# Linear attention in a two-layer backbone: the key-value product of each head on its own 64 columns of TensorE, both heads at the same PSUM columns

## The chip, the cores and the metric

The kernel runs on one core of a Trainium2 chip. The metric is device time in microseconds from the first to the last instruction of the program, with the small fixed part around them; a run's time is compared with other runs on the same chip. TensorE (PE) multiplies, VectorE (DVE) and ScalarE (ACT) work elementwise and read PSUM, GpSimd (POOL) works elementwise in SBUF, SyncE (SP) issues most of the loads.

## The reference, cut to what matters

Two layers over 512 latent and 256 context tokens. Each layer is a half-step feed-forward network, a token mixer and a second feed-forward network. One branch of the mixer is gated linear attention with 4 heads (key width 64, value width 128), in chunks of 64 tokens, forwards and backwards:

```python
kv = jnp.einsum('bhncd,bhnce->bhnde', k_end, vc)      # per head and chunk: (64 x 64 tokens) x (64 tokens x 128)
decay = jnp.exp(b_last[:, :, :, 0, :])

def step(s, inp):
    kv_n, dec_n = inp
    return s * dec_n[..., None] + kv_n, s
```

The state of a head is 64 x 128 numbers. The chain of 12 chunks (8 of the latent, 4 of the context) is walked in order, so each state needs the one before it.

## The kernel before

All values are float32. The large products (feed-forward, projections) are split into a high and a low part in float32r (`whi`, `wlo`, `hhi`, `hlo`) and run at lines 1261 and 1268. One "unit" is 128 output columns over all tokens. The attention's small products are plain float32; each such `matmul` appears in the trace as two MATMUL and two LDWEIGHTS records.

Attention handles the heads in two pairs (`pr` 0 and 1), for each of 2 layers. Head `h` of the pair lies on partitions 64h to 64h+63 of `states`, `dec` and `kt`. A pair needs `KV_STEPS` = 11 state steps. In step `s`, for each of the 2 directions `d`:

- `kv_products` on PE multiplies the two heads' keys of one chunk (`kpad`, 128 columns: 64 for each head) with the two heads' values (`vt`, 256 columns: 128 for each head). Of the 128 x 256 result only two blocks are wanted: head 0's keys with head 0's values (partitions 0 to 63, columns 0 to 127), and head 1's with head 1's (partitions 64 to 127, columns 128 to 255). The other half is computed and never read.
- `state_step` on DVE makes the next state from each block, with one instruction for each head and direction: 4 per step. They are line 1070 for `s` = 0 and line 1072 after it.

PSUM is double-buffered: step `s` uses bank `s % 2`, so PE may run two steps ahead of DVE and then waits for `kv_used`. The other attention products are the scores (`scores`, line 692, masked by DVE at 1054 and 1055), the outputs (`outputs`, line 712, copied by ACT at 906) and transposes of values (line 605, drained by DVE's `copy_v` at 1006) and of decayed keys (line 672, drained by ACT at 879 and 880).

The order is written out by hand for each engine. On PE the small products are a generator, `gla_tensor`, whose pieces are placed by `gla_slot` between the k-chunks of 8 large units, `fill_tensor`. Each engine executes in program order, so a PE piece that waits also holds the large units behind it. On DVE, `gla_vector` puts between the state steps: `scale_keys` (1047, `kt`), `scale_queries` (1029, `qbd`), `copy_v`, `mask_scores` and the split of the next unit's weights (1703, `wlo`). For pair 1, `scores(1, 0)` is PE's next attention piece after `kv_products(1, 7)` and waits for the last of the four `scale_queries`, which DVE issues after state step 6.

Of the kernel before, what the change touches and what calls it, by code (L numbers as in the profile page):

```python
# [21 lines left out]
P = 128  # L22
# [9 lines left out]
DK = 64  # L32
DV = 128
# [38 lines left out]
ALU = mybir.AluOpType  # L72
# [88 lines left out]
def blocks(l):  # L161
    return NBLK if l < DEPTH - 1 else XBLK


def gla_slot(l, kind, pr=0, i=0):


    lead, chain, out = (5, (1.3, 1.8), 1.5) if l < DEPTH - 1 else (8, (1.6, 2), 2)
    chains = [lead + 4, 0]
    outs = [chains[0] + chain[0] * KV_STEPS + 1, 0]  # L170
    chains[1] = outs[0] + 2 * out * blocks(l) + 1
    outs[1] = chains[1] + chain[1] * KV_STEPS + 1
    if kind == "kend":
        return lead + i / 2 if pr == 0 else outs[0] + 2 * out * (1 + i / 2) + out / 2
    if kind == "kv":
        return chains[pr] + chain[pr] * i
    if kind == "o":
        return outs[pr] + 2 * out * i
    assert kind == "var"
    return outs[1] + 2 * out * (2 + i if i < 2 else blocks(l) + i / 2)  # L180
# [13 lines left out]
def build(nc, t):  # L194
# [87 lines left out]
    vt = lay("vt", [P, NBLK, VW])  # L282
    kq = lay("kq", [P, 4, NT])
    states = lay("states", [P, 2, NCH, DV])
    bsum = lay("bsum", [P, 4, NT])
    qbd = lay("qbd", [P, 2, 2, NT])
    kpad = lay("kpad", [P, 2, NBLK, 2, P])
# [6 lines left out]
    dec = lay("dec", [P, 2, NCH])  # L294
# [31 lines left out]
    ps = ctx.enter_context(nc.psum_tensor("ps", [P, 8 * 512], F32))  # L326

    def bank(b, c0=0, n=512):
        return ps[:, 512 * b + c0:512 * b + c0 + n]
# [115 lines left out]
    def at_least(eng, s, value):  # L445

        if not isinstance(value, int) or value > 0:
            eng.wait_ge(s, value)
# [199 lines left out]
    def o_before(l, pr):  # L648

        return 2 * sum(blocks(i) for i in range(l)) + pr * blocks(l)  # L650
# [8 lines left out]
    def gla_tensor(pe, l, p0):  # L659
# [15 lines left out]
        def kv_products(pr, s):  # L675

            kv0 = (2 * l + pr) * KV_STEPS
            at_least(pe, kv_used, kv0 + s - 1)
            for d, order in enumerate((FWD, BWD)):
                c = order[s]  # L680
                mm = nc.tensor.matmul(bank(s % 2, d * 2 * P, 2 * P), kpad[:, d, c // 2, c % 2, :],  # L681
                                      vt[:, c // 2, 2 * pr * DV:2 * (pr + 1) * DV], start=True, stop=True)
            mm.then_inc(kv_ready, 1)

        def scores(pr, b):
# [318 lines left out]
    def copy_v(dve, l, g):  # L1004
        dve.wait_ge(misc_ready, MISC * l + 5 + g)
        nc.vector.tensor_copy(vt[:, :, g * DV:(g + 1) * DV],
                              bank(6, 0, NT).rearrange("p (b n) -> p b n", b=NBLK)).then_inc(misc_free, 1)

    def to_end(dve, l, pr):

        dve.wait_ge(b_ready, 4 * l + 2 * pr + 2)
        if pr:
            dve.wait_ge(eq_ready, 4 * l + 2)
        for d in range(2):
            b = bsum[:, 2 * pr + d, :].rearrange("p (n c) -> p n c", c=CHUNK)
            e = (CHUNK - 1, 0)[d]
            nc.vector.tensor_tensor(kend(pr)[:, d, :].rearrange("p (n c) -> p n c", c=CHUNK),
                                    b[:, :, e:e + 1].to_broadcast([P, NCH, CHUNK]), b, ALU.subtract).then_inc(d_ready, 1)

    def scale_kend(dve, l, pr):  # L1020
        for d in range(2):
            dve.wait_ge(eend_ready, 4 * l + 2 * pr + d + 1)
            nc.vector.tensor_tensor(kend(pr)[:, d, :], kq[:, pr, :], kend(pr)[:, d, :], ALU.mult).then_inc(kend_ready, 1)

    def scale_queries(dve, l, pr, d, h):
        c = blocks(l) * P
        dve.wait_ge(eq_ready, 4 * l + 2 * pr + d + 1)
        r = slice(h * DK, (h + 1) * DK)
        ins = nc.vector.tensor_tensor(qbd[r, d, h, 0:c], kq[r, 2 + pr, 0:c], qbd[r, d, h, 0:c], ALU.mult)
        if h:  # L1030
            ins.then_inc(prep_ready, 1)

    def gla_vector(dve, steps, l, u0, split_lo):
        nb = blocks(l)
        done = 0

        def fill_to(slot):

            nonlocal done
            while done < FILL and SLOTS * (done + 1) + 1 <= slot:  # L1040
                unit = u0 + AHEAD + done + 2
                split_lo(unit, unit % 4, unit % 2)
                done += 1

        def scale_keys(pr, d):
            dve.wait_ge(ekt_ready, 4 * l + 2 * pr + d + 1)
            nc.vector.tensor_tensor(kt[:, d, :], kq[:, pr, :], kt[:, d, :], ALU.mult)

        def mask_scores(pr, b):
            ob = o_before(l, pr)  # L1050
            dve.wait_ge(s_ready, ob + b + 1)

            at_least(dve, o_ready, ob + b - 1)
            steps.link(nc.vector.copy_predicated(att[:, b % 2, :], masks[:, 0, :], bank(6 + b % 2, 0, 2 * P)))
            nc.vector.copy_predicated(att[:, b % 2, :], masks[:, 1, :],
                                      bank(6 + b % 2, 2 * P, 2 * P)).then_inc(att_ready, 1)

        def state_step(pr, s):
            kv0 = (2 * l + pr) * KV_STEPS
            dve.wait_ge(kv_ready, kv0 + s + 1)  # L1060
            if s:
                dve.wait_ge(kv_used, kv0 + s)
            for d, order in enumerate((FWD, BWD)):
                ch, nxt = order[s], order[s + 1]
                for h in range(2):
                    r = slice(h * DK, (h + 1) * DK)
                    col = 512 * (s % 2) + d * 2 * P + h * DV
                    kv = ps[r, col:col + DV]
                    if s == 0:
                        ins = nc.vector.tensor_copy(states[r, d, nxt, :], kv)  # L1070
                    else:
                        ins = nc.vector.scalar_tensor_tensor(  # L1072
                            out=states[r, d, nxt, :], in0=states[r, d, ch, :], scalar=dec[r, d, ch:ch + 1],
                            in1=kv, op0=ALU.mult, op1=ALU.add)
            ins.then_inc(kv_used, 1)

        unit = u0 + AHEAD + 1
        split_lo(unit, unit % 4, unit % 2)
        scale_keys(0, 0)
        scale_queries(dve, l, 0, 1, 0)  # L1080
        scale_queries(dve, l, 0, 1, 1)
        dve.wait_ge(dec_ready, 2 * l + 1)
        for s in range(KV_STEPS):
            fill_to(gla_slot(l, "kv", 0, s))
            state_step(0, s)
            if s == 1:
                scale_keys(0, 1)
            if s in (2, 3):
                copy_v(dve, l, s)
            if s in (5, 6):  # L1090
                mask_scores(0, s - 5)
        to_end(dve, l, 1)
        for b in range(2, nb):
            fill_to(gla_slot(l, "o", 0, b - 1.5))
            mask_scores(0, b)
            if b == 2:
                scale_kend(dve, l, 1)
        fill_to(gla_slot(l, "o", 0, nb - 1))
        dve.wait_ge(o_ready, o_before(l, 0) + nb)
        dve.wait_ge(dec_ready, 2 * l + 2)  # L1100
        for s in range(KV_STEPS):
            fill_to(gla_slot(l, "kv", 1, s))
            state_step(1, s)
            if s in (1, 2):
                scale_keys(1, s - 1)
            if 3 <= s <= 6:
                scale_queries(dve, l, 1, (s - 3) // 2, (s - 3) % 2)
            if s == 8:
                mask_scores(1, 0)
        mask_scores(1, 1)  # L1110
        for b in range(2, nb):
            fill_to(gla_slot(l, "o", 1, b - 1.5))
            mask_scores(1, b)
        fill_to(gla_slot(l, "var", 1, HEADS - 1))
        dve.wait_ge(ostd_ready, l + 1)
        v = tok[:].rearrange("p (h b) -> p h b", h=HEADS)[:, :, 0:nb]
        nc.vector.reciprocal(v, v).then_inc(orec_ready, 1)
        fill_to(NEVER)
# [1079 lines left out]
```

## Time and profile before

| | |
|---|---|
| median of 3 runs | 3025.59 us (3024.77 to 3027.01) |
| profiled execution, its own time | 3025.89 us |
| its span | 3024.1 us |
| PE busy | 2961.8 us (98%) |
| DVE busy | 1599.1 us (53%) |
| ACT, POOL busy | 830.5 us (27%), 259.6 us (9%) |
| state step instructions (1070 and 1072) | 16 + 160, 288 and 348 ns median |
| key-value MATMUL records (681) | 176, 379 ns median |

A record's duration is its own, from start to end; consecutive matmuls overlap, so what a matmul costs PE is the distance from one start to the next. Only where PE is idle inside a stretch does the work of another engine reach the end of the program. Attention of layer 0 lies at 716 to 860 us of the span, that of layer 1 at 2345 to 2460 us.

### The profile page before, as it was taken

How to read it: one execution, taken by the hardware profiler on the slowest of the kernel's cores; microseconds unless marked ns; L12 is line 12 of the kernel's file. 1: busy time of each engine (PE TensorE's matmuls, PEld its weight loads, DVE VectorE, ACT ScalarE, POOL GpSimd, SP SyncE). 2: the span in 40 equal slices, each digit the busy share in tenths (PEclk: the TensorE clock that was granted, in tenths of full speed). 3: DMA queues.
4: the chain of work that ended last, by engine and by line, in shares of the span. 5: the costliest groups of instructions: out<-in, count | busy, mean ns of one | idle time of the engine just before them, and what ended most of it. 6: DMA issues, size and time to landing. Idle time of an engine off the chain costs nothing.

```text
span 3024.1 us, 41524 instructions
## 1 busy us (share of the span) xinstructions
PE 2961.8 (98%) x16228; PEld 2537.2 (84%) x16228; DVE 1599.1 (53%) x2658; ACT 830.5 (27%) x1142; POOL 259.6 (9%) x260
## 2 busy tenths in 40 slices
PE   7999999999999999999999999999999899999998
PEld 5888888888888888888888888888888688888886
DVE  6676776557443348776765752222245744433333
ACT  4211211243232232212112421121234333432223
POOL 2000000112600020000000200000021500200001
PEclk8999999999999999999999999999999999999998
DMA  6444334222012224434442432222113123333331
GB/s 215 119 118 133 118 112 140 70 59 50 25 49 62 70 70 134 137 112 132 118 133 70 119 91 63 63 62 63 53 40 85 39 65 96 91 96 92 98 94 65
DMA packets 455618, 273.64 MB, mean 90 GB/s; under 512 B 9754, under 2 KB 453828, under 8 KB 455492
## 3 DMA queue, kind: packets, MB, share of 16 engines
q1 hardware_dynamic: 453348, 267.90, 31.1%
q10 hardware_dynamic: 2144, 4.00, 0.4%
q8 instruction: 87, 1.43, 0.2%
q14 instruction: 39, 0.32, 0.0%
HBM read 269.77 MB, written 2.10 MB: 90 GB/s over the span
## 4 chain that ended last, share of the span: by engine, by line
PE 91%; DVE 4%; ACT 2%; issue 1%; DMA 0%; SPq 0%; POOL 0%; DVEq 0%; ACTq 0%; POOLq 0%
PE ps L1261 54%; PE ps L1268 27%; PE ps L1436 2%; PE ps L1284 2%; PE ps L1441 1%; DVE states L1072 1%; PE ps L712 1%; PE ps L1318 1%; PE ps L681 1%; DVE first_acc L1770 1%; PE ps L692 1%; ACT hhi L1601 0%; DMA first_mod<-in_w_mod 0%; DVE hlo L1826 0%; PE ps L596 0%
## 5 line engine op out<-in xcount | busy, mean ns | idle before, releaser
L1261 PE MATMUL ps<-hhi,whi 128*128 128x512 f32 x3136 | 890.7, 351 | 0.2 <-ACT whi L1530 0.2
L1261 PE MATMUL ps<-hlo,whi 128*128 128x512 f32 x3136 | 879.6, 348 | 0.0
L1703 DVE TENSOR_TENSOR wlo<-wraw,whi 128x1024 fp32r<-128x1024 f32 x371 | 456.8, 1232 | 594.1 <-ACT whi L1530 591.4
L1530 ACT ACTIVATE whi<-wraw 128x1024 fp32r<-128x1024 f32 x371 | 391.4, 1056 | 932.6 <-PE ps L1268 908.3
L1268 PE MATMUL ps<-hhi,wlo 128*128 128x512 f32 x3136 | 629.9, 350 | 0.0
L1261 PEld LDWEIGHTS ps<-hhi,whi 128*128 128x128 f32 x3136 | 501.3, 188 | 82.4 <-issue 3.1
L1268 PEld LDWEIGHTS ps<-hhi,wlo 128*128 128x128 f32 x3136 | 501.5, 188 | 80.6 <-issue 1.0
L1261 PEld LDWEIGHTS ps<-hlo,whi 128*128 128x128 f32 x3136 | 500.3, 188 | 79.8 <-issue 0.5
L1717 DVE SCALAR_TENSOR_TENSOR macc<-modraw,cond,macc 128x256 f32<-128x256 f32 x896 | 366.2, 478 | 0.1
L1261 PE MATMUL ps<-mhi,whi 128*128 128x512 f32 (+1 forms) x1184 | 333.8, 349 | 4.2 <-DVE mlo L1967 2.9
L1261 PE MATMUL ps<-mlo,whi 128*128 128x512 f32 (+1 forms) x1184 | 332.2, 348 | 0.0
L1963 DVE TENSOR_TENSOR mtmp<-ps,stmp 128x512 f32<-128x512 f32 (+1 forms) x154 | 82.6, 572 | 303.6 <-ACT stmp L1654 303.6
L1268 PE MATMUL ps<-mhi,wlo 128*128 128x512 f32 (+1 forms) x1184 | 234.5, 348 | 0.0
L1654 ACT ACTIVATE stmp<-ps 128x512 f32<-128x512 f32 (+1 forms) x154 | 70.8, 505 | 555.6 <-PE ps L1268 555.6
L1261 PEld LDWEIGHTS ps<-mhi,whi 128*128 128x128 f32 x1184 | 188.8, 188 | 37.3 <-DVE mlo L1967 5.0
L1268 PEld LDWEIGHTS ps<-mhi,wlo 128*128 128x128 f32 x1184 | 189.0, 188 | 30.6
L1261 PEld LDWEIGHTS ps<-mlo,whi 128*128 128x128 f32 x1184 | 188.9, 188 | 30.3
L2111 POOL MEMSET ssq<- 128x768 f32 x7 | 5.2, 741 | 2225.4 <-PE ps L1268 1856.1
L1977 DVE SCALAR_TENSOR_TENSOR x<-ps,gate,x 128x512 f32<-128x512 f32 (+3 forms) x156 | 89.9, 635 | 148.1 <-PE ps L1268 148.1
L1967 DVE TENSOR_TENSOR mlo<-mtmp,mhi 128x768 f32 (+3 forms) x88 | 78.5, 892 | 91.2 <-ACT mhi L1658 91.2
L1658 ACT ACTIVATE mhi<-mtmp 128x768 f32 (+3 forms) x88 | 69.8, 793 | 107.9 <-DVE mtmp L1963 107.9
L2021 POOL TENSOR_TENSOR ssq<-ssq,sq 128x768 f32<-128x768 f32 (+2 forms) x52 | 83.6, 1609 | 164.6 <-ACT sq L1555 81.5
(193 smaller groups left out, 2377.8 us busy)
## 6 DMA issues: line engine op xcount, KB each, us to landing
wraw<-in_ffn_up SPq DMA_DIRECT2D x176, 512.0 KB, 3.9
modraw<-in_w_mod SPq DMA_DIRECT2D x66, 1024.0 KB, 5.2
wraw<-in_ffn_down SPq DMA_DIRECT2D x64, 512.0 KB, 3.7
wraw<-in_w_in SPq DMA_DIRECT2D x64, 512.0 KB, 4.0
wraw<-in_ffn_down SPq DMA_DIRECT2D x32, 384.0 KB, 3.3
wraw<-in_w_out SPq DMA_DIRECT2D x16, 512.0 KB, 3.7
first_mod<-in_w_mod SPq DMA_DIRECT2D x6, 1024.0 KB, 12.5
wraw<-in_w_br_pool SPq DMA_DIRECT2D x16, 256.0 KB, 2.8
```

The source lines that it names most:

```text
L1261: nc.tensor.matmul(o, whi[:, slot, k, :], a[:, k * NT + t0:k * NT + t0 + n], start=(k == 0 and a is hi), stop=False)
L1268: mm = nc.tensor.matmul(o, wlo[:, slot, k, :], hi[:, k * NT + t0:k * NT + t0 + n], start=False, stop=k == kk - 1)
L1284: mm = nc.tensor.matmul(o, w[:, (unit + s) % 2, k, :], h[:, k * NT + t0:k * NT + t0 + n], start=(k == 0 and w is whi and h is hhi and open ...
L1530: nc.scalar.activation(whi[:, slot2], wraw[:, slot4], ACT.Copy).then_inc(hi_split, 1)
L1654: ins = nc.scalar.activation(stmp[:, h, pt[0]:pt[0] + pt[1]], pair_ps(buf, 0, pt), ACT.Silu)
L1658: nc.scalar.activation(mhi[:, ds((2 * i + h) * NT, c)], mtmp[:, h, 0:c], ACT.Copy).then_inc(mhi_done, 1)
L1703: nc.vector.tensor_tensor(wlo[:, slot2], wraw[:, slot4], whi[:, slot2].bitcast(F32), ALU.subtract).then_inc(lo_split, 1)
L1717: ins = nc.vector.scalar_tensor_tensor(out=macc[:, buf, c, :], in0=modraw[:, buf, k, :], scalar=cond[:, c * DC + k:c * DC + k + 1], in1=ma ...
L1963: ins = nc.vector.tensor_tensor(mtmp[:, h, pt[0]:pt[0] + pt[1]], pair_ps(buf, 1, pt), stmp[:, h, pt[0]:pt[0] + pt[1]], ALU.mult)
L1967: nc.vector.tensor_tensor(mlo[:, ds((2 * i + h) * NT, c)], mtmp[:, h, 0:c], mhi[:, ds((2 * i + h) * NT, c)].bitcast(F32), ALU.subtract).th ...
L1977: ins = nc.vector.scalar_tensor_tensor(out=x[:, ds(n * NT + t0, m)], in0=pair_ps(buf, s, (t0, m)), scalar=gate[:, ds(e * DC + n, 1)], in1= ...
L2021: nc.gpsimd.tensor_tensor(ssq[:, t0:t0 + c], ssq[:, t0:t0 + c], sq[:, j % 2, t0:t0 + c], ALU.add).then_inc(sq_used, 1)
```

## The change

On PE, the product of a direction becomes two, one for each head: 64 of the key columns with that head's own 128 value columns, written to that head's 64 partitions of PSUM, at the same 128 columns for both heads. On DVE, both blocks of a direction then lie at the same columns on all 128 partitions, and one instruction handles both heads.

```diff
@@ kv_products
             for d, order in enumerate((FWD, BWD)):
                 c = order[s]
-                mm = nc.tensor.matmul(bank(s % 2, d * 2 * P, 2 * P), kpad[:, d, c // 2, c % 2, :],
-                                      vt[:, c // 2, 2 * pr * DV:2 * (pr + 1) * DV], start=True, stop=True)
+                for h in range(2):
+                    r = slice(h * DK, (h + 1) * DK)
+                    mm = nc.tensor.matmul(bank(s % 2, d * DV, DV)[r], kpad[:, d, c // 2, c % 2, r],
+                                          vt[:, c // 2, (2 * pr + h) * DV:(2 * pr + h + 1) * DV], start=True, stop=True)
             mm.then_inc(kv_ready, 1)
@@ state_step
                 ch, nxt = order[s], order[s + 1]
-                for h in range(2):
-                    r = slice(h * DK, (h + 1) * DK)
-                    col = 512 * (s % 2) + d * 2 * P + h * DV
-                    kv = ps[r, col:col + DV]
-                    if s == 0:
-                        ins = nc.vector.tensor_copy(states[r, d, nxt, :], kv)
-                    else:
-                        ins = nc.vector.scalar_tensor_tensor(
-                            out=states[r, d, nxt, :], in0=states[r, d, ch, :], scalar=dec[r, d, ch:ch + 1],
-                            in1=kv, op0=ALU.mult, op1=ALU.add)
+                kv = bank(s % 2, d * DV, DV)
+                if s == 0:
+                    ins = nc.vector.tensor_copy(states[:, d, nxt, :], kv)
+                else:
+                    ins = nc.vector.scalar_tensor_tensor(
+                        out=states[:, d, nxt, :], in0=states[:, d, ch, :], scalar=dec[:, d, ch:ch + 1],
+                        in1=kv, op0=ALU.mult, op1=ALU.add)
             ins.then_inc(kv_used, 1)
```

DVE in layer 0, pair 1, from state step 0 to the last `scale_queries`, before (`states` and `kt`, `qbd` are the tiles that are written; 64x128 is partitions by columns; x4 is four instructions in a row):

```order
L1070 COPY states<-ps 64x128 x4
L1072 SCALAR_TENSOR_TENSOR states<-states,dec,ps 64x128 x4
L1047 TENSOR_TENSOR kt<-kq,kt 128x768
L1072 SCALAR_TENSOR_TENSOR states<-states,dec,ps 64x128 x4
L1029 TENSOR_TENSOR qbd<-kq,qbd 64x768
L1703 TENSOR_TENSOR wlo<-wraw,whi 128x1024
```

The same rows of the change:

```order
L1069 COPY states<-ps 128x128 x2
L1071 SCALAR_TENSOR_TENSOR states<-states,dec,ps 128x128 x2
L1049 TENSOR_TENSOR kt<-kq,kt 128x768
L1071 SCALAR_TENSOR_TENSOR states<-states,dec,ps 128x128 x2
L1031 TENSOR_TENSOR qbd<-kq,qbd 64x768
L1702 TENSOR_TENSOR wlo<-wraw,whi 128x1024
```

Nothing changes its place in the order; every state step is two instructions on 128 partitions where it was four on 64.

PE in layer 0, pair 0, around state steps 1 to 3, before (64x128 or 128x256 is the result, partitions by columns):

```order
L1261 MATMUL ps<-hlo,whi 128x256
L681 MATMUL ps<-vt,kpad 128x256 x4
L605 MATMUL ps<-ident,vf 128x128 x6
L1261 MATMUL ps<-hhi,whi 128x512
L681 MATMUL ps<-vt,kpad 128x256 x2
```

The same rows of the change:

```order
L1260 MATMUL ps<-hlo,whi 128x256
L683 MATMUL ps<-vt,kpad 64x128 x8
L605 MATMUL ps<-ident,vf 128x128 x6
L1260 MATMUL ps<-hhi,whi 128x512
L683 MATMUL ps<-vt,kpad 64x128 x4
```

A step's two matmuls become four, each with half the moving columns and half the stationary ones, between the same neighbours, all of which use the full 128 x 128 array.

## Rows read from the trace of the kernel before

**Rows 1.** The page: its head, and the chain that ended last, by engine.
```profile
span 3024.1 us, 41524 instructions
...
PE 91%; DVE 4%; ACT 2%; issue 1%; DMA 0%; SPq 0%; POOL 0%; DVEq 0%; ACTq 0%; POOLq 0%
```

**Rows 2.** Timeline of PE, layer 0 pair 1: start, duration, instructions, [idle before <-releaser].
```profile
781.86 1.13 PE L681 MATMUL ps<-vt,kpad 128*128 128x256 f32 x4 [0.18 <-DVE states L1072]
...
786.09 1.13 PE L681 MATMUL ps<-vt,kpad 128*128 128x256 f32 x4 [1.70 <-DVE states L1072]
...
788.42 1.13 PE L681 MATMUL ps<-vt,kpad 128*128 128x256 f32 x4 [0.51 <-DVE states L1072]
792.06 1.46 PE L692 MATMUL ps<-qbd,kt 128*128 128x256 f32 x4 [2.50 <-DVE qbd L1029]
792.96 3.12 PE L1268 MATMUL ps<-hhi,wlo 128*128 128x512 f32 x8
...
796.66 1.06 PE L1268 MATMUL ps<-hhi,wlo 128*128 128x512 f32 x4
```

**Rows 3.** Stretch after them: busy PE, PEld, DVE, ACT, POOL, clock, DMA.
```profile
792.00:796.70 4.70, 4.64 (x17) 3.97 (x17) 1.33 (x4) 0.00 (x0) 3.88 (x12) 0.64 0.01 2
```

**Rows 4.** Timeline of DVE, layer 0 pair 1.
```profile
774.22 1.43 DVE L1072 SCALAR_TENSOR_TENSOR states<-states,dec,ps 64x128 f32<-64x128 f32 x4 [0.98 <-PE ps L681]
775.69 1.70 DVE L1047 TENSOR_TENSOR kt<-kq,kt 128x768 f32<-128x768 f32 x1
...
788.40 0.98 DVE L1029 TENSOR_TENSOR qbd<-kq,qbd 64x768 f32<-64x768 f32 x1
...
790.74 1.18 DVE L1029 TENSOR_TENSOR qbd<-kq,qbd 64x768 f32<-64x768 f32 x1
```

**Rows 5.** Line 1072, who waited for it: us in all, times (whole program).
```profile
  PE ps L681: 5.6, 7
```

**Rows 6.** Timeline of PE, its other idle times in the two attention stretches.
```profile
726.97 0.87 PE L605 MATMUL ps<-ident,vf 128*128 128x128 f32 x6 [1.86 <-DVE vt L1006]
...
752.74 0.52 PE L672 MATMUL ps<-ident,bsum 128*128 128x128 f32 x3 [0.45 <-DVE bsum L1023]
...
2356.19 0.88 PE L605 MATMUL ps<-ident,vf 128*128 128x128 f32 x6 [2.11 <-DVE vt L1006]
...
2373.88 0.71 PE L712 MATMUL ps<-att,vt 128*128 128x128 f32 x4 [2.27 <-DVE states L1072]
...
2412.72 1.10 PE L692 MATMUL ps<-qbd,kt 128*128 128x256 f32 x4 [2.82 <-DVE qbd L1029]
```

**Rows 7.** Timeline of DVE, layer 1 pair 1: step 1, last query scaling.
```profile
2396.72 1.43 DVE L1072 SCALAR_TENSOR_TENSOR states<-states,dec,ps 64x128 f32<-64x128 f32 x4
...
2410.92 1.65 DVE L1029 TENSOR_TENSOR qbd<-kq,qbd 64x512 f32<-64x512 f32 x1
```

**Rows 8.** The chain that ended last, in order of time: start, duration, what.
```profile
737.92 0.86 PE ps L681 x4
738.78 0.70 PE ps L1268 x4
```

**Rows 9.** Timeline of PE around products on 32 columns (128*32), line 1342.
```profile
203.21 0.52 PE L1268 MATMUL ps<-mhi,wlo 128*128 128x512 f32 x2
203.65 0.28 PE L1342 MATMUL ps<-mred,fold 128*32 128x24 f32 x8
203.86 0.62 PE L1261 MATMUL ps<-mhi,whi 128*128 128x512 f32 x2
204.31 0.52 PE L1261 MATMUL ps<-mlo,whi 128*128 128x512 f32 x2
204.67 0.52 PE L1261 MATMUL ps<-mhi,whi 128*128 128x512 f32 x2
```

**Rows 10.** Timeline of DVE before the first state step.
```profile
715.71 0.95 DVE L1047 TENSOR_TENSOR kt<-kq,kt 128x768 f32<-128x768 f32 x1
716.58 1.91 DVE L1029 TENSOR_TENSOR qbd<-kq,qbd 64x768 f32<-64x768 f32 x2
```

## The prediction

> **What bounds the kernel now.** I read the page first: the chain that ended last is 91% PE and 4% DVE [rows 1]. PE is therefore the bound nearly everywhere, and an edit to DVE counts only where PE stands idle for it. Then I asked for the line of the state steps and who waits for it: PE's key-value products wait 5.6 us in 7 places [rows 5]. That is only the direct part, so I went through PE's timeline in both attention stretches for each idle time, and through DVE's for what made it late.
>
> In layer 0, pair 1, PE waits 0.18, 1.70 and 0.51 us for line 1072 and 2.50 us for the scaled queries [rows 2], 4.9 us together. DVE has no gap from 774.22 to 791.92 us [rows 4], and in that stretch lie the state steps 1 to 6, at 1.43 us each. Layer 1, pair 1 looks the same: of the 5.6 us in 7 places [rows 5], what is left after the three of layer 0 is 3.2 us, in four places. To it comes 2.82 us before the scores [rows 6], 6.0 us together, while DVE is occupied from 2396.72 to 2412.57 us, again with six state steps inside [rows 7]. Four further idle times stand in [rows 6]: 1.86 and 2.11 us for the copy of transposed values, 0.45 us for a scaled key, and 2.27 us for the last state of pair 0 in layer 1. All of PE's idle time that has DVE behind it is thus 4.9 + 6.0 + 1.86 + 0.45 + 2.11 + 2.27 = 17.6 us.
>
> One more cost hangs on it. Right after the 2.50 us wait the granted clock averages 0.64 over 792.0 to 796.7 us [rows 3], so part of that stretch runs at 1.2 instead of 2.4 GHz. From the start of the scores at 792.06 to 796.66 us [rows 2] PE does four records of scores, eight of line 1268 and four of key-value products. At full clock these take 0.86 + 1.40 + 0.86 = 3.1 us (a key-value group of four is 0.86 and four of line 1268 are 0.70 [rows 8]; the scores have the form of the key-value products). It took 4.6 us, so the slow clock costs 1.4 to 1.5 us. Layer 1 has the same shape after its 2.82 us wait, and I put it at 1.4 us too.
>
> **DVE: four instructions become two.** 1.43 us for four is 0.358 us each. The new ones have the same 128 columns but twice the partitions. Does that cost time? 128x768 took 0.95 us, and two of 64x768 took 1.91 us, 0.955 each [rows 10]: partitions cost nothing. So a step falls from 1.43 to 0.72 us, by 0.72 us.
>
> A bound on the better side: the instructions of [rows 10] overlap, the second starts at 716.58, 0.08 us before the first ends at 716.66, whereas the state instructions stand 0.358 us apart with durations of 0.348. If the new pair and its successor overlap as those do, another 0.1 us is gained at each of two places, and a step saves 0.9 us. The Trainium skill (VectorE: DVE Perf Modes, section Two Vector instructions with no wait between them) says that an instruction is held until all earlier ones have finished when its operands start in another quadrant of partitions than those of the instruction before. The old steps alternate between partitions 0 and 64 and would all be held, the new ones would not; by the page the saving would be about 0.9 us, by the bare count of instructions 0.72. I take between 0.72 and 0.9, nearer to the count, since a step's first instruction also follows a wait.
>
> What this is worth, place by place:
> - Layer 0 pair 1: six steps save 4.3 to 5.4 us of DVE's chain; PE's idle time there is 4.9 us, and the fresh weight load after each of four waits adds 0.1 (1.13 instead of about 1.03 us). I take 4.6.
> - Layer 1 pair 1: six steps again, 6.0 us of idle time: 4.6.
> - The two waits for copied values, 1.86 and 2.11 us: state steps 1 and 2 lie on DVE between the first products and the copy, 1.43 to 1.8 us saved. I take 1.5 each, 3.0.
> - The last state of pair 0, layer 1, 2.27 us: the last four steps follow each other on DVE almost without gap and would save 2.9 us. All of the wait goes, 2.3 with its weight load.
> - The scaled key, 0.45 us: it is late by the last state step (0.7 us shorter). I take 0.4.
> - The clock: remaining waits before the scores would be 1 us or less in layer 0 and about 1.5 in layer 1. At 2.11 and 2.27 us [rows 6] no slow stretch follows in this trace, only after 2.50 and 2.82. So I count both stretches as gone, 2.8 us.
>
> Sum: 4.6 + 4.6 + 3.0 + 2.3 + 0.4 + 2.8 = 17.7 us.
>
> **PE: two matmuls become four on half the columns.** Before, a step costs 0.86 us for four records of 256 columns, 0.215 each [rows 8], so 128 columns are 0.107. After it there are eight records of 128 columns. One after another they are 0.86 us again. If the two 64-column halves of the array work side by side, they are 0.43; if records start in program order, with head 0's two and then head 1's two, a head's first can only run beside the other's second, and a step is five times 0.107, 0.54.
>
> To this comes going to half the array and back. The trace has the nearest case in line 1342 [rows 9], eight records on 32 columns between full-array products. A pair of large matmuls is normally 0.36 us (204.31 to 204.67), so line 1342 should have started at 203.57 and started at 203.65: 0.08 to 0.09 to get in. From there to line 1261 it is 0.21. Back on the full array the first pair takes 0.45 instead of 0.36: 0.09. In all 0.39 us, of which the 24 moving columns can hardly be more than 0.04 when side by side. Eight loads and eight products one after another would be 8 x (32 + 24) columns at 0.84 ns, 0.38 us, and they and the way out took 0.21: the column groups do overlap. The rest, 0.35 us, I take for the two switches, plus 0.03 for loading 64 columns first instead of 32.
>
> The Trainium skill (TensorEngine Tiling (Array Packing), section Tiling Modes, Key Properties) says both things: changing the tiling mode drains TensorE, which speaks against this change, and tiles load and multiply in parallel, which speaks for it. By these rows the trace agrees with both.
>
> So a step costs 0.38 plus 0.43, 0.54 or 0.86 us: 0.81, 0.92 or 1.24, against 0.86. I take 0.92, since that is what in-order starts give: +0.06 us, 2.6 us over 44 steps. Some 12 steps lie where PE waits for DVE anyway and hides it, which leaves 2 us. If that cover were gone the full 2.6 would count. Nothing else changes: no load, no other wait, and no instruction moves past another.
>
> Total: 17.7 - 2 = 15.7 us. Against the profiled execution, 3025.89 - 15.7 = 3010.2; its time is 0.3 above the median, so 3010 us.
>
> **The rivals.**
> - **The halves of the array do not overlap.** The float32 records of one head then follow those of the other, and a step costs 1.24 us, +0.38. With 32 steps in the open that is 12.2 us, and 17.7 - 12.2 = 5.5 gained: 3020. Against it stands line 1342 [rows 9], but with 32 columns and short products. Chance 0.12.
> - **The gain is passed on to another wait.** PE comes to each later place earlier, and ACT's drains of the transposed keys or GpSimd (which slows DVE's kt to 1.70 us where 0.95 is usual [rows 4, 10]) now hold it; and one of the slow stretches of the clock stays or comes elsewhere. If half of the DVE terms (7.5) and one slow stretch (1.4) are lost, the gain is 6.8: 3019. For it speaks that layer 1 pair 1 keeps 1.5 us of waiting even by my count. Chance 0.08.
> - **Slower: weight loads are exposed.** If with half the columns each load has to wait for the product in front of it, each of a step's eight adds 0.05 us (half of the 0.1 seen after a wait [rows 2]). A step costs 0.38 + 0.86 + 0.43 = 1.67 us, +0.81; over 32 steps 26 us, less 17.7: 3034. This ends above the old time as soon as a step costs more than 17.7 / 32 = 0.55 us extra. The Trainium skill (TensorE: Matmul & The Clock Gate, Part 3, What overlaps and what doesn't) has loads overlap running products only when their row groups differ, and here they are the same; the full-array rows, all with the same row group, already contradict it, with a float32 product of 128 columns and its load at 0.107 us. Chance 0.06.
> - **More than forecast.** Side-by-side halves (0.81 a step, 2 us better than before), state steps at 0.9 and all 17.6 us of waits gone: 17.6 + 1 + 2.8 + 2 = 23.4, 3002. Chance 0.12, at the edge of my own case.
>
> **How the numbers follow.** My case, 3004 to 3016, has 0.62 and gives the forecast of 3010. The 3002 case and the two cases at 3019 and 3020 are taken into the range, 3002 to 3020; the exposed loads and what lies beyond the others are left out. 0.2% is 6 us, about what a measurement of this kernel can tell from no change, so faster means below 3019.5. My case, the better one and half of the two weaker ones give 0.84; the other half gives 0.10 for no change; slower has 0.06.
>
> **What would show it.** The state steps of the changed kernel should stand as x2 on 128 partitions at about 0.35 us each, 0.7 a step or less. The 2.50 and 2.82 us waits before the scores should be below 1 and 1.6 us, and the wait for the last state of pair 0 in layer 1 gone. The clock should read 1.00 after them. A step of key-value products between two large ones should cost PE about 0.92 us from start to start; 1.24 would show the first rival, 1.6 the third. The prediction is wrong if that distance is above 1.4, or if PE's waits name ACT where they named DVE.

## The result, and the profile after

The changed kernel took 2999.49 us (median of 4 runs, 2998.74 to 3000.08), the kernel before, beside it, 3026.24 us (4 runs, 3024.77 to 3027.01). The ratio is 0.9911, 95% interval 0.9899 to 0.9923: 26.8 us or 0.9% faster. The forecast was 15.7 us faster and its range ended at 3002: right in direction and outside the range by 2.5 us.

The page of the changed kernel, head and chain by engine (line numbers are one lower or two higher than before):

```profile
span 2997.0 us, 41788 instructions
...
PE 93%; DVE 3%; ACT 2%; issue 1%; DMA 0%; SPq 0%; POOL 0%; DVEq 0%; ACTq 0%; POOLq 0%
```

DVE's share of the chain fell from 4% [rows 1] to 3%, and PE's grew from 91% to 93% of a shorter span. The next view is PE's timeline of the changed kernel, its idle times in the attention stretches (they answer [rows 2, 6]):

```profile
724.56 0.88 PE L605 MATMUL ps<-ident,vf 128*128 128x128 f32 x6 [0.42 <-DVE vt L1008]
...
749.77 0.52 PE L672 MATMUL ps<-ident,bsum 128*128 128x128 f32 x3 [0.45 <-ACT kpad L882]
...
783.19 1.10 PE L694 MATMUL ps<-qbd,kt 128*128 128x256 f32 x4 [0.57 <-DVE qbd L1031]
...
2342.04 0.87 PE L605 MATMUL ps<-ident,vf 128*128 128x128 f32 x6 [0.51 <-DVE vt L1008]
...
2388.98 1.10 PE L694 MATMUL ps<-qbd,kt 128*128 128x256 f32 x4 [1.57 <-DVE qbd L1031]
```

The waits of 2.50 and 2.82 us before the scores are now 0.57 and 1.57; the copies of values went from 1.86 and 2.11 to 0.42 and 0.51; the wait for the last state, 2.27 us, has no row any more. PE's key-value products have no wait for a state left in the trace, where they had seven, 5.6 us together [rows 5]. Only the 0.45 us at line 672 is as before, and there the name has changed: it was DVE's `bsum`, it is now ACT's `kpad`.

To see where the time went, both attention stretches are cut from the first transposed key (line 672) to the first spread of the norm (line 780, now 782). Stretches by window, PE alone: length, busy, records, clock, DMA. First the kernel before, then the changed one:

```profile
713.93:857.03 143.10, 135.45 (x791) 0.99 0.13 32
2344.31:2455.06 110.75, 98.99 (x495) 0.98 0.17 41
```

```profile
713.85:846.33 132.48, 130.59 (x878) 1.00 0.14 35
2332.29:2429.53 97.24, 93.68 (x584) 1.00 0.18 47
```

The two together went from 253.9 to 229.7 us: 24.1 of the 27.1 us by which the spans differ. PE's idle time in them went from 19.4 to 5.5 us. What is left, 3.0 us, lies outside, where both programs are the same. One thing that differs there is the clock. Two windows in other phases, in the kernel before and then in the changed one:

```profile
1675.00:1690.00 15.00, 15.00 (x105) 0.89 0.01 1
2238.00:2260.00 22.00, 22.00 (x131) 0.84 0.04 8
```

```profile
1675.00:1690.00 15.00, 14.99 (x98) 1.00 0.54 150
2238.00:2260.00 22.00, 21.97 (x147) 1.00 0.00 1
```

The windows do not hold quite the same work, but no slow stretch of the clock shows near these places in the changed kernel (1.00 over 1650 to 1700 and over 2205 to 2250 us). At a mean of 0.84 over 22 us, 3.5 us' worth of clock is missing, and at 0.89 over 15 us another 1.7. The 3.0 us are a net figure, though. The changed kernel leaves the attention of layer 0 10.7 us ahead (857.03 against 846.33) and is only 8.4 us ahead 200 us later (PE's rows at 1057.13 and 1048.70). It then gains 1.6 and 3.1 us where the two slow stretches are missing, loses 1.0 in other places, and enters the attention of layer 1 12.0 us ahead (2344.31 against 2332.29). The last 1.6 us are gained behind that. Most of the 2.3 us goes where the large products follow each other at another rate: by their starts from 950 to 1040 us, about 0.174 us a record in the kernel before and 0.176 to 0.177 in the changed one. No run here explains that.

The new pair of state instructions, DVE's timeline (it answers [rows 4]):

```profile
770.90 0.61 DVE L1071 SCALAR_TENSOR_TENSOR states<-states,dec,ps 128x128 f32<-128x128 f32 x2 [1.60 <-PE ps L683]
771.43 1.50 DVE L1049 TENSOR_TENSOR kt<-kq,kt 128x768 f32<-128x768 f32 x1
```

Two instructions take 0.61 us, and the next starts 0.08 us before they end, 0.53 us after the first began. The four of before held DVE for 1.47 us (774.22 to 775.69). A step saves 0.94 us. And the step of products, from the chain that ended last (it answers [rows 8]) and PE's timeline:

```profile
736.71 0.59 PE ps L683 x8
737.30 0.89 PE ps L1267 x4
```

```profile
735.15 0.66 PE L683 MATMUL ps<-vt,kpad 128*64 128x128 f32 x8
735.74 0.97 PE L1267 MATMUL ps<-hhi,wlo 128*128 128x512 f32 x4
736.64 0.66 PE L683 MATMUL ps<-vt,kpad 128*64 128x128 f32 x8
```

The period is 1.49 us with four records of line 1267, which need 0.70 behind full-array products [rows 8] and 0.89 behind half-array ones. With everything above 0.70 put down to the step, it costs 0.79 us: 0.07 less than the 0.86 of before, where the forecast said 0.06 more.

### The profile page after: what moved, and what is told of

It reads as the page before. It is cut to its first block, busy times and chain, and to the rows that moved or that the text cites. A ratio compares the mean times of both kernels' runs of the same rounds, so it can differ in the third digit from the quotient of the medians.

```text
span 2997.0 us, 41788 instructions
## 1 busy us (share of the span) xinstructions
PE 2949.3 (98%) x16404; PEld 2515.6 (84%) x16404; DVE 1563.6 (52%) x2570; ACT 830.4 (28%) x1142; POOL 262.6 (9%) x260
## 4 chain that ended last, share of the span: by engine, by line
PE 93%; DVE 3%; ACT 2%; issue 1%; DMA 0%; SPq 0%; POOL 0%; DVEq 0%; ACTq 0%; POOLq 0%
PE ps L1260 55%; PE ps L1267 28%; PE ps L1435 2%; PE ps L1283 2%; PE ps L1440 1%; PE ps L714 1%; PE ps L694 1%; DVE first_acc L1769 1%; PE ps L1317 1%; PE ps L683 1%; ACT hhi L1600 0%; DMA first_mod<-in_w_mod 0%; DVE hlo L1825 0%; PE ps L596 0%; DVE x L1976 0%
## 6 DMA issues: line engine op xcount, KB each, us to landing
first_mod<-in_w_mod SPq DMA_DIRECT2D x6, 1024.0 KB, 12.2
```

## The experiments

Each was run beside the kernel before on the same chip. "Attention" is the sum of the two stretches cut as above, from PE's timeline in that kernel's profile (before 253.9, changed 229.7). It comes from one execution of each kernel, while the times are medians.

**The PE half alone.** DVE keeps four instructions; each head keeps its own PSUM columns.

```diff
-                mm = nc.tensor.matmul(bank(s % 2, d * 2 * P, 2 * P), kpad[:, d, c // 2, c % 2, :],
-                                      vt[:, c // 2, 2 * pr * DV:2 * (pr + 1) * DV], start=True, stop=True)
+                for h in range(2):
+                    r = slice(h * DK, (h + 1) * DK)
+                    mm = nc.tensor.matmul(bank(s % 2, d * 2 * P + h * DV, DV)[r], kpad[:, d, c // 2, c % 2, r],
+                                          vt[:, c // 2, (2 * pr + h) * DV:(2 * pr + h + 1) * DV], start=True, stop=True)
```

> Only the PE half of the change: two matmuls per direction on 64 columns each, but each head keeps its own PSUM columns and DVE its four instructions per step. Theory A (the changed trace: a step costs PE 0.79 us where it was 0.86, and nearly all the rest of the gain is DVE's): 32 steps in the open times 0.07 is 2.4 us, so 3022 to 3025 us, with the waits for states as long as before and both slow clock stretches in attention still there. Theory B (PE's part is a large share of the 27 us): below 3018. The prediction's own term (0.92 a step, 2 us lost): 3028.

3028.49 us (10 runs, 3021.14 to 3033.07), ratio 1.0003 (0.9993 to 1.0012): no difference. Both theories missed; the 3028 of the prediction's own term is met by luck, since a step costs 0.79 us and not the 0.92 behind it. In the profiled execution (3029.7 us, above the median) attention took 259.2 us, 5 us more than before, although each step of products is as short as in the change. The windows of the two stretches in this kernel:

```profile
714.18:859.13 144.95, 135.65 (x878) 0.95 0.13 32
2344.67:2458.87 114.20, 99.73 (x584) 0.94 0.16 40
```

PE is idle 23.8 us here against 19.4 before: DVE's chain sets the time, and a faster PE only waits longer. And the clock is lower: 2 x (0.05 x 145 + 0.06 x 114) is some 28 us at 1.2 GHz, against 7 before. PE's busy time is 235.4 us, where the changed kernel needs 224.3 for the same 878 and 584 records, 11 us less. At half speed 28 us cost 14, but some 5 of the 28 fall on waits and cost nothing there (from 789.5 to 796.5 us the clock is 0.51 and PE is busy for 4.0 of 7.0 us), which leaves 11 to 12. Against before, 4.4 us went into waits, and the 3 that the steps save were more than eaten by the clock.

**The DVE half alone.** PE keeps its two products of 128 x 256. The one instruction per direction reads the first 128 columns on all 128 partitions, so head 1's state is made from head 0's values: the computation is changed there, and the work has the same size.

```diff
-                for h in range(2):
...
-                        ins = nc.vector.scalar_tensor_tensor(
-                            out=states[r, d, nxt, :], in0=states[r, d, ch, :], scalar=dec[r, d, ch:ch + 1],
-                            in1=kv, op0=ALU.mult, op1=ALU.add)
+                kv = bank(s % 2, d * 2 * P, DV)
...
+                    ins = nc.vector.scalar_tensor_tensor(
+                        out=states[:, d, nxt, :], in0=states[:, d, ch, :], scalar=dec[:, d, ch:ch + 1],
+                        in1=kv, op0=ALU.mult, op1=ALU.add)
```

> Only the DVE half: PE's products as before (128 x 256), DVE two instructions of 128 partitions per step. For head 1 it reads head 0's value columns, so the states of head 1 are computed from the wrong block; amounts of work are those of the change. Theory A: everything but PE's 2 to 3 us is here, 3001 to 3004 us, a state step takes 0.60 us, waits before the scores below 2 us. Theory B (the two halves work only together, or PE's part is large): 3010 or more.

3003.87 us (4 runs, 2998.51 to 3007.58), ratio 0.992 (0.9903 to 0.9937): theory A. Attention is 232.9 us (PE busy for 228.6 of it). The DVE half is 20.9 of the 24.1 us there, and the PE half, worth nothing alone, adds 3.2 on top of it: close to 44 x 0.07. That is read from profiles; the intervals of the two times (0.9903 to 0.9937 and 0.9899 to 0.9923) overlap.

**Both heads on the same half of the array.**

```diff
-                    mm = nc.tensor.matmul(bank(s % 2, d * DV, DV)[r], kpad[:, d, c // 2, c % 2, r],
+                    mm = nc.tensor.matmul(bank(s % 2, d * 2 * P + h * DV, DV)[0:DK], kpad[:, d, c // 2, c % 2, r],
```

> The change, but both heads' products go to the same 64 columns of the array (partitions 0 to 63 of PSUM, side by side in columns), so that they cannot run beside each other; DVE's instructions are those of the change and for head 1 read partitions that no product has written. Theory A (the two halves of the array run fully beside each other, eight records in 0.43 us): here they are one after another, a step costs PE about 1.22 instead of 0.79 us, and with 32 of 44 steps in the open the time is 3011 to 3016. Rival (short products are not bound by the array, so no overlap was gained): within 2 us of the change, 2998 to 3002.

3018.69 us (9 runs, 3014.53 to 3020.49), ratio 0.997 (0.996 to 0.998). PE's timeline:

```profile
739.00 1.09 PE L683 MATMUL ps<-vt,kpad 128*64 128x128 f32 x8
740.02 0.97 PE L1267 MATMUL ps<-hhi,wlo 128*128 128x512 f32 x4
740.91 1.09 PE L683 MATMUL ps<-vt,kpad 128*64 128x128 f32 x8
```

The period is 1.91 us, so a step costs 1.21: 0.42 more than in the change, which is 4 x 0.107. Attention is 245.1 us, 15.4 more. The halves run fully side by side in the change, and without that two thirds of the gain would be gone: this is the first rival of the prediction (3020), made on purpose. DVE reads partitions here that no product has written, so the results differ and the work does not.

**PE's two loops exchanged.**

```diff
-            for d, order in enumerate((FWD, BWD)):
-                for h in range(2):
+            for h in range(2):
+                for d, order in enumerate((FWD, BWD)):
```

> The change with PE's two loops exchanged: both directions of head 0 first, then both of head 1. Theory A, in the strict form that records start in program order (behind the prediction's 0.54): four records of one half stand ahead of the first of the other, a step costs about 7 x 0.107 + 0.36 = 1.11 us, 3008 to 3012. Rival (each half takes its own records as it comes free, as the records 7 ns apart in the trace of the change suggest): 0.79 as in the change, 2998 to 3001.

3003.74 us (4 runs, 2998.19 to 3007.71), ratio 0.9915 (0.9899 to 0.9932), the same as the change within the intervals. Its timeline shows the step of the change, not the 1.11 us of starts in program order:

```profile
736.48 0.66 PE L683 MATMUL ps<-vt,kpad 128*64 128x128 f32 x8
737.07 0.97 PE L1267 MATMUL ps<-hhi,wlo 128*128 128x512 f32 x4
737.97 0.66 PE L683 MATMUL ps<-vt,kpad 128*64 128x128 f32 x8
```

**The same eight records on the full array.** The DVE half as above, and PE's product cut by value columns alone; head 1's state is again made from head 0's values.

```diff
+                for h in range(2):
+                    mm = nc.tensor.matmul(bank(s % 2, d * 2 * P + h * DV, DV), kpad[:, d, c // 2, c % 2, :],
+                                          vt[:, c // 2, (2 * pr + h) * DV:(2 * pr + h + 1) * DV], start=True, stop=True)
```

> As the change, two matmuls per direction with 128 moving columns each, but on all 128 stationary columns, so the array is never divided; DVE as in the change, reading head 0's value columns for both heads (head 1's states are computed from the wrong block). Theory A (the switch in and out of the half array costs 0.36 us a step, in the change's step of 0.79 and the one-half step of 1.21): a step costs PE 0.86 us, the time is that of the DVE half alone, 3001 to 3005. Rival (the number of records costs): above 0.95 a step, 3006 or more.

3003.28 us (4 runs, 3000.74 to 3004.46), ratio 0.9916 (0.99 to 0.9933). PE's timeline:

```profile
736.36 1.05 PE L682 MATMUL ps<-vt,kpad 128*128 128x128 f32 x8
737.17 0.94 PE L1266 MATMUL ps<-hhi,wlo 128*128 128x512 f32 x4
737.95 1.05 PE L682 MATMUL ps<-vt,kpad 128*128 128x128 f32 x8
```

Period 1.59, a step 0.89 us, and attention 233.6, like the DVE half alone. Three prices follow: eight records one after another 0.86 to 0.89; with the array divided and no overlap 1.21, so going in and out costs 0.32 to 0.35; with overlap 0.79. Running the halves side by side saves 0.43 us a step, and dividing the array costs a third of a microsecond.

**DVE's two loops exchanged, on the kernel before.**

```diff
-            for d, order in enumerate((FWD, BWD)):
-                ch, nxt = order[s], order[s + 1]
-                for h in range(2):
-                    r = slice(h * DK, (h + 1) * DK)
+            for h in range(2):
+                r = slice(h * DK, (h + 1) * DK)
+                for d, order in enumerate((FWD, BWD)):
+                    ch, nxt = order[s], order[s + 1]
```

> The kernel before with DVE's two loops exchanged: head 0's two directions, then head 1's two, four instructions as before. Theory A (an instruction starts before the end of the one ahead only when both start at the same partition): two of the four places overlap by 0.09 us, a step takes 1.26 instead of 1.43 us; two stretches of six steps give 1.0 us each and the rest 0.5, so 3023 to 3025, a slow clock stretch less perhaps. Rival (the 0.60 us of the new pair comes from something else): 1.43 a step, 3025 to 3028.

3019.67 us (7 runs, 3017.12 to 3021.47), ratio 0.9973 (0.9961 to 0.9984): 7 us for an exchange of two lines, where theory A gave 1 to 3. DVE's timeline:

```profile
738.11 1.24 DVE L1072 SCALAR_TENSOR_TENSOR states<-states,dec,ps 64x128 f32<-64x128 f32 x4
```

1.24 us where four took 1.43: two of the three seams inside a step now join instructions that start at the same partition, and each is 0.08 to 0.1 us shorter. Attention fell by 5.1 us to 248.8. Its slow clock did not shrink: in windows of half a microsecond the clock is at 1.2 GHz for 6.8 us of attention, as in the kernel before.

**Longer waits on the full array, and half-array products with shorter waits.** These two ask why the clock was so low in the attention of the PE half alone. The first is the kernel before with two short instructions more in each step on DVE:

```diff
+                        if h == 0:
+                            nc.vector.scalar_tensor_tensor(
+                                out=spare[r, d, :], in0=states[r, d, ch, 0:8], scalar=dec[r, d, ch:ch + 1],
+                                in1=kv[:, 0:8], op0=ALU.mult, op1=ALU.add)
```

> The kernel before, with two more short instructions of 8 columns on DVE in every state step after the first (their result goes to a spare tile), about 0.2 us each: a step takes DVE some 1.8 to 1.9 us instead of 1.43, PE still uses the whole array. What is asked is why the PE half alone was so slow although its step is 0.07 us shorter: its granted clock in attention was at 1.2 GHz for 27 us instead of 7. Theory A (longer waits of PE for the states bring the slow stretches, whatever form the products have): the waits grow by 0.4 us for each of some 16 steps on DVE's chain, and slow stretches in attention multiply, 3035 to 3040. Theory B (the half-array products bring the slow clock): waits grow but the slow stretches stay at about two, 3031 to 3034.

3036.86 us (5 runs, 3035.1 to 3040.87), ratio 1.0042 (1.0028 to 1.0056). A step takes DVE 1.7 us. The clock over 700 to 865 us is 0.98 and over 2330 to 2460 us 0.97, some 14 us of slow clock: twice that of before, half that of the PE half alone, whose waits for states are as long (7.3 and 7.5 us for products). The start of one of its steps on DVE also bears on the seams:

```profile
777.55 0.34 DVE L1073 SCALAR_TENSOR_TENSOR states<-states,dec,ps 64x128 f32<-64x128 f32 x1 [0.97 <-PE ps L682]
777.82 0.21 DVE L1077 SCALAR_TENSOR_TENSOR spare<-states,dec,ps 64x8 f32<-64x8 f32 x1
778.04 0.71 DVE L1073 SCALAR_TENSOR_TENSOR states<-states,dec,ps 64x128 f32<-64x128 f32 x2
```

The short instruction begins at the partition of the one before it and starts 0.07 us before that one ends; the next begins at partition 64 and starts only when the short one has ended.

The second is the PE half alone with DVE's loops exchanged as above.

> The PE half of the change with DVE's four instructions in the order of the heads (1.24 instead of 1.43 us a step): half-array products with shorter waits. Theory A (waits bring the slow clock): slow stretches in attention like those of the kernel before or fewer, and the gain over the PE half alone is more than the 7 us that this order gave on the kernel before, 3014 to 3020. Theory B (half-array products bring it): the slow stretches stay near 27 us in attention, 3021 or more.

3017.26 us (10 runs, 3015.6 to 3020.54), ratio 0.9972 (0.9962 to 0.9981), inside theory A's range. That is the ratio of the exchange on the kernel before (0.9973): the PE half was worth nothing once more, as long as PE waits for DVE. Against the PE half alone (1.0003) the exchange gave 0.3%, or 9 us, which is not clearly more than the 0.27% on the kernel before. Attention is 248.3 us, its mean clock 0.99 and 0.97.

What the profiles say of the clock is best seen side by side: PE's waits for DVE in attention, and the time at 1.2 GHz there in windows of half a microsecond:

| products | kernel | waits for DVE | at 1.2 GHz |
|---|---|---|---|
| full array | DVE's loops exchanged | 12.5 us | 7 us |
| full array | before | 17.7 us | 7 us |
| full array | two more instructions | 20.9 us | 14 us |
| half array | DVE's loops exchanged | 16.3 us | 10 us |
| half array | PE half alone | 21.9 us | 27 us |

The kernels with the longest waits have the most slow clock with either form of product, so that theory A holds in direction. Where half-array products were set beside full-array ones with about the same waits there was more of it, a half more in one case and twice as much in the other, so the form may count as well. One profile each does not separate the two.

**The change again, and what it still waits for.**

> The changed kernel itself once more, in more rounds. What is asked is how much of the 27 us is steady. In its first profile 24 us of the gain lie in the two attention stretches and 2.7 us outside them, where the program is the same and only slow clock stretches differ. Theory A (the part outside is chance, it depends on where the slow stretches fall): the runs spread over some 5 us from 2998 up, and the time moves with the mean granted clock, median 2999 to 3003. Theory B (the part outside belongs to the change): all runs at 2998.5 to 3000.5 as the first four.

3000.04 us (4 runs, 2998.29 to 3001.56), ratio 0.9909 (0.9892 to 0.9925). The result lies between the two theories. The profile gives attention 229.8 us and a span of 2997.6. So the 24 us in attention repeat exactly, and the part outside was there both times: 2767.8 us after 2767.3, against 2770.3 before. The other kernels show how far that part can be trusted; see below.

```diff
-                if s in ((4, 5), (7, 9))[pr]:
+                if s in ((4, 5), (8, 9))[pr]:
```

> The change, with the first scores of pair 1 placed behind state step 8 instead of 7 on PE, DVE unchanged. Theory A (the 0.57 and 1.7 us that PE still waits there are DVE being late with the scaled queries): both waits go and 1.5 to 2.3 us are gained, 2997 to 2998. Rival (DVE then waits for the later scores and PE's outputs for DVE): no gain, 2999 to 3001.

2997.18 us (4 runs, 2994.78 to 2997.66), ratio 0.9897 (0.9881 to 0.9914). Both waits before the scores are gone and attention is 227.5 us, 2.2 less. The intervals of the two times overlap. Run again beside the change:

> The kernel with the later scores of pair 1 again, beside the change on the same chip. Theory A: 2 us below the change. Rival: no difference beyond 1 us.

2997.33 us (4 runs, 2996.07 to 3000.81), ratio 0.9898 (0.9882 to 0.9915), against 3000.04 and 0.9909 of the change, attention 227.5 again. The 2.2 us in attention repeat; the times point the same way without telling the two kernels apart. And, with that edit kept, the copy of values ahead of a scaling on DVE:

```diff
             state_step(0, s)
-            if s == 1:
-                scale_keys(0, 1)
             if s in (2, 3):
                 copy_v(dve, l, s)
+            if s == 2:
+                scale_keys(0, 1)
```

> The change with the later scores of pair 1, and in pair 0 on DVE the copy of transposed values ahead of the second scaling of keys (0.95 us). PE's waits of 0.4 to 0.5 us for that copy in both layers should go. Theory A: 1 us below the kernel with later scores alone. Rival: the second copy or the first scores of pair 0 now wait instead: no difference.

2995.76 us (4 runs, 2993.87 to 2997.9), ratio 0.9897 (0.988 to 0.9913). The waits at line 605 are gone. This is the lowest median of all kernels run, 4 us under the change's; its interval overlaps the change's (0.9892 to 0.9925), so that these microseconds lie inside what the runs can tell. Its profile does not bear theory A out: attention is 229.5 us, 2 more than with the later scores alone, with a slow stretch of the clock in layer 0 (mean 0.97 over 134.4 us), and the low time of that execution (a span of 2992.1 us) comes from outside attention.

## Why the prediction was right and wrong

**Right: the place.** PE's idle times in [rows 2, 6] were the gain. The terms for them were 14.9 us; PE's idle time in attention fell by 14.0. By place: 4.6 was said for pair 1 of layer 0 and 4.9 - 0.57 = 4.3 us of waiting went; 4.6 in layer 1, and 6.0 - 1.57 = 4.4 went; 3.0 for the copies, and 3.0 went; 2.3 for the last state, all of it. Only the 0.4 for the scaled key was wrong: that wait is still 0.45 us, with ACT's drain of the transposed keys behind it. It is the one place where the prediction's own sign of being wrong, ACT named where DVE was named, came true. Partitions cost nothing, as said: the 128-partition instruction has a median of 343 ns, the 64-partition one had 348.

**Mis-sized: the state step.** I took nearly the bare count, 0.72 us; a step saves 0.94. The trace of before already had it in [rows 10], and the exchanged loops show the cause: instructions that start at the same partition overlap by 0.08 to 0.1 us, those that alternate between partitions 0 and 64 do not. The prediction's other estimate, 0.9 us, came from the rule of the Trainium skill that a Vector instruction is held until the earlier ones have finished when it starts in another quadrant, a group of 32 partitions (VectorE: DVE Perf Modes, section Two Vector instructions with no wait between them), and the trace agrees with it. It mattered little for the places above, since there the waits themselves limit what can be gained: the places came out within half a microsecond each.

**Failed: the term for PE.** The prediction said "I take 0.92, since that is what in-order starts give: +0.06 us, 2.6 us over 44 steps", 2 us in the open. Measured is 0.79 us, -0.07, about -3.1 us: 5 us of the 11 that were missed. The 0.38 us for the switches was nearly right (0.32 to 0.36), the side-by-side value 0.43 was right, and it was the choice between 0.43 and 0.54 that failed. With the loops exchanged, four records of one head stand ahead of all of the other, and the step does not change: the halves do not hold each other up. Starts in program order, on which the 0.92 rests, are not what the traces show between the two halves: 0.79 us a step with either order of the loops.

**Right in attention, silent outside it: the clock.** Both slow stretches in attention went, as counted. They were worth 3.4 us and not 2.8: 6.8 us at 1.2 GHz, in two places (around 794 and 2416 us), all of it with PE busy. Outside attention 3.0 us more came that the sum did not have. No instruction there is changed. The second run of the same kernel had it too, but that is not enough to give it to the change. The kernel with the later scores is one program with two profiles, and outside attention it took 2767.5 us in one and 2771.5 in the other, on another chip; over all profiled kernels of this record, none of which changes anything outside, that part takes from 2762.6 to 2773.1 us. The kernel with PE's loops exchanged has the slow stretches back at both places (a clock of 0.96 over 1660 to 1700 and 0.94 over 2205 to 2260 us). So these 3 us are as likely luck as an effect of the change.

So of the 11 us missed, 5 are the PE term, 3 lie outside attention, and 3 in attention on DVE's side: the DVE half alone gave 20.9 us there against 17.7 counted. Its windows say where. PE's idle time fell by 15.0 us, which is what the terms for idle time had (14.9). PE's busy time fell by 5.9 us, where the sum had only the 2.8 of the clock: the clock gave 0.6 more than that, and 2.5 us come from elsewhere in PE's work. The weight loads behind each wait (0.1 us each [rows 2], for the ten waits that went) would make 1.0 of these, by estimate; the rest was not resolved.

**The rivals.** No overlap did not occur; made on purpose it costs 12.2 us in attention against undivided products (245.1 and 232.9), the 12.2 that the rival had, and the time is 3018.7 where it had 3020. Exposed weight loads did not occur: a step costs 0.79 us, and 1.21 even without overlap, not 1.67 (where the working says 0.43 for eight times 0.05 it should be 0.40, which changes nothing). Passing on the gain did not occur to any size: PE's waits for ACT's `kpad` went from 1.6 us in three places to 2.1 in four, the fourth being the scaled key's. "More than forecast", 3002 with 0.12, came nearest, and it too ended above the result: it had 0.81 us for a step and nothing for what PE's busy time and the parts outside attention gave. A range whose lower edge assumes that every named term goes well has still to leave room for what isn't named, here several microseconds either way for phases that the edit does not touch.

## What to carry to other kernels

Halving the number of instructions on the engine that is waited for is worth its chain time even at 53% busy; measure it from start to start, and look at which partition neighbouring instructions begin. Making the bound engine's work shorter where it waits for another is worth nothing (1.0003 alone, and 0.9972 against 0.9973 with DVE's loops exchanged), and by the profiles the same edit gains 3 us in attention once the wait is gone: judge two halves of a change together. When a gain shows in a phase that the edit does not touch, look at other profiles of that phase before counting it. Small products on half the stationary columns pay if both halves get work at once; a visit to the half array costs about 0.35 us here, so it needs more than that in saved streaming.

## What the runs showed that was not expected

The PE half alone made PE's step shorter and, in the execution that was profiled, attention 5 us longer, with some 28 us at 1.2 GHz where there were 7; over ten runs the kernel's time did not change. And the order of two Python loops on DVE, with the same instructions, was worth 7 us (0.9973), because it decides which instructions start at the same partition as the one before.
